# Two chained networks on one core: modulation weights taken in groups of four 2048-column units, and eight units of layer two moved behind the first expert stage

## The chip, the cores and the metric

One core of one Trainium2 chip runs the whole program in one launch. The metric is the device time of that launch in microseconds, the median of several runs. All arithmetic is in 32-bit floating point, apart from one clearing of accumulators in bf16.

## The reference, cut to what matters

256 tokens of width 1024 pass through a network of two layers and then through a second network. Each layer first makes a modulation vector from a condition vector `c`, and uses its six parts as shifts, scales and gates:

```python
for layer in range(2):
    mod = silu(c) @ w_ada[layer] + b_ada[layer]          # 1024 x 6144
    sh1, sc1, g1, sh2, sc2, g2 = split(mod, 6)
    h = rms_norm(x, norm1_g[layer]) * (1 + sc1) + sh1
    mix = (dilated attention | spatial gating)(h)        # layer 0, weights ev_*
          (causal convolution | stick-breaking attention)(h)  # layer 1, weights od_*
    x = x + g1 * mix
    h = rms_norm(x, norm2_g[layer]) * (1 + sc2) + sh2
    x = x + g2 * experts(h)        # 16 experts, top 2 of one group per token
x = rms_norm(x, final_norm_g)
```

The second network has a modulation of its own (`w_c`, 1024 x 3072), a 1024 x 8192 input projection `w_in`, a gated recurrence, a neighbourhood attention and three output projections.

## The kernel before, in words

**The ring.** All large weights pass through a ring of six SBUF slots (`RING`, L34), each holding one unit of 4096 floats per partition, 2 MB (2,097,152 bytes). `stream()` (L99) lists the units in order; SyncE fetches them in that order (L407 to L445). Unit n goes into slot n % 6 and its fetch waits until unit n - 6 has been read (`read_wait`, L278). A unit of `ada`, `ev`, `od` or `in` is 512 columns wide over all 1024 rows (`layout`, L419), so that each partition receives eight pieces of 2 KB. An expert unit gives each partition one piece of 16 KB.

**The modulation.** 30 `ada` units (24 of `w_ada`, 6 of `w_c`) are computed one by one. Most are done by TensorE: `ada_main` (L510) makes 8 products of 512 columns, four of them side by side on 32 columns of the array each (recorded as 16 matmuls, since an fp32 product is two), into one PSUM bank. This bank holds 4 partial sums, each repeated on 32 partitions. ScalarE copies the bank to SBUF (`ada_part_copy`, L1228); `ada_columns` (L534) adds over the partitions and turns row into column with four products with a column of ones (8 recorded matmuls), and VectorE scales by 1/32 and adds the bias (`ada_cols`, L1759). Ten units (4 to 11, 28, 29; `SUMMED`, L118) are instead summed by VectorE, `modulate` (L1767): eight multiply-adds of 512 columns per unit; `summed_columns` (L546) makes their columns.

**Stage one** is everything ahead of the first expert loop. It fetches 30 units in this order: ada 0 to 3; ev0; ada 4; ev1; ada 5, 6; ev2; ada 7; ev4; ada 8; ev3; ada 9 to 17; evo0, evo1; ada 18 to 22. TensorE's order is written out by hand: four `ada_main` with their columns (L613 to L632), the projections ev0, ev1, ev2 (L950 to L955), then eight attention heads (`heads`, L700): in each head the scores of the next head, the transposes of this head's probabilities (`turn`), and the value products (`values`). Head 0 holds ev4 ahead of its `turn`, head 1 holds ev3 and `summed_columns(8, 12)`. Heads 1 to 6 hold one `ada_main` between `turn` and `values` (`beside_turned`, L980) and one `ada_columns` behind `values` (`after_a`, L984): ada 12 to 17. Then follow evo0, evo1, two `ada_main`, and the routing of the experts.

**The routing** (`experts`, L714 to L763) is a chain between TensorE and VectorE (`route`, L1931). TensorE fills its waits: `units - 3` times `ada_main` and two `ada_columns` behind the logits, one `ada_main` and two (layer one) or one (layer two) `ada_columns` behind the rank products, and only then the product that counts tokens left over (L753) and the first `gather`.

**The expert loop** takes pairs of experts, six units per pair; the same in both layers.

**Stage two**, behind the first loop: od0, od1, od2, od3, od4, ada 23, odo0, odo1, ada 24 to 27. VectorE meanwhile runs the 31 taps of a causal convolution (`taps`, L2320) on od0 and od1. GpSimd sends the gate and two modulation rows through DRAM as 4-byte elements (`broadcast_gate`, L2584, `affine_by_row`, L2570): in layer one once 6 and 10 units are ready (L2643 to L2645), in layer two both right after unit 18 and the gain (L2661 to L2664).

## Time and profile before

| | us |
|---|---|
| median of 3 runs | 1254.09 |
| lowest and highest run | 1247.88, 1258.9 |
| span of the profiled execution | 1250.4 |
| TensorE busy in it | 1181.6 (94%) |
| VectorE, ScalarE, GpSimd busy | 417.0, 289.5, 83.6 |
| mean granted TensorE clock | 0.977 |
| DMA moved | 352.78 MB, mean 282 GB/s |

The span runs from the first to the last instruction of one execution taken by the profiler; no other time of that execution is given. PE is TensorE's matmul stream, PEld its weight loads, DVE VectorE, ACT ScalarE, POOL GpSimd, SP SyncE. L491 is a projection by channel, L504 one by token, L529 the products of `ada_main`, L542 those of `ada_columns`, L805 the experts' products, L777 the gather. A row names what ended the idle time before it behind `<-`.

### The profile page before, as it was taken

What the parts mean: (1) busy time and instruction counts of PE and PEld (TensorE: products, weight loads), DVE (VectorE), ACT (ScalarE), POOL (GpSimd) and SP (SyncE); (2) the same over time, 40 slices, a digit from 0 to 9 for tenths busy, and PEclk for the clock granted to TensorE, in tenths of its full rate; (3) what the DMA queues carried; (4) which work ended last, traced back from release to release, by engine and by line L of the source; (5) the groups of instructions that cost most, each with busy time, mean ns of one, the idle gap of its engine ahead of it and who ended that gap; (6) DMA issues with size and microseconds to landing.
All of it is one profiled execution on the core that took longest, in us unless ns stands there. A gap on an engine that the chain in (4) does not pass through costs nothing.

```text
span 1250.4 us, 17188 instructions
## 1 busy us (share of the span) xinstructions
PE 1181.6 (94%) x6994; PEld 696.9 (56%) x6995; DVE 417.0 (33%) x1096; ACT 289.5 (23%) x616; POOL 83.6 (7%) x141
## 2 busy tenths in 40 slices
PE   4979999999999989999989999998999999999997
PEld 1746644544444438764534443444877787767783
DVE  0456724322212123962521211114521243342222
ACT  2201433111000022063310001103002455452101
POOL 0200011000000001500000000000000223200000
PEclk8989889899999999999899999999999999999999
DMA  9999998899999999731769999999595334334000
GB/s 339 348 349 303 386 295 339 322 423 430 428 429 428 429 398 234 232 142 68 317 244 424 429 428 429 429 428 389 186 272 173 116 113 156 101 131 141 7 18 34
DMA packets 90372, 352.78 MB, mean 282 GB/s; under 512 B 5284, under 2 KB 7500, under 8 KB 78028
## 3 DMA queue, kind: packets, MB, share of 16 engines
q1 hardware_dynamic: 83160, 340.68, 72.2%
q0 software_dynamic: 5488, 8.12, 3.0%
q10 hardware_dynamic: 1668, 3.21, 0.7%
q8 instruction: 38, 0.62, 0.2%
q14 instruction: 18, 0.15, 0.0%
HBM read 350.84 MB, written 1.15 MB: 281 GB/s over the span
## 4 chain that ended last, share of the span: by engine, by line
PE 72%; DMA 20%; DVE 3%; ACT 2%; issue 1%; SPq 1%; DVEq 0%; ACTq 0%
PE bank L491 26%; PE bank L805 19%; DMA ring<-in_moe_w_up 12%; PE bank L504 10%; DMA ring<-in_w_ada 6%; PE bank L777 3%; DMA ring<-in_ev_w_out 2%; PE bank L826 2%; PE bank L529 2%; PE bank L1070 1%; DVE arena L1598 1%; SPq L401 1%; PE bank L542 1%; PE bank L655 1%; PE bank L692 1%
## 5 line engine op out<-in xcount | busy, mean ns | idle before, releaser
L491 PE MATMUL bank<-arena,ring 128*128 128x256 f32 x1600 | 353.6, 382 | 2.3 <-ACT arena L1163 1.7
L805 PE MATMUL bank<-ring,arena 128*32 128x512 f32 x3072 | 336.3, 595 | 10.3 <-issue 4.6
L491 PEld LDWEIGHTS bank<-arena,ring 128*128 128x128 f32 x1600 | 303.8, 191 | 49.3 <-issue 6.6
L805 PEld LDWEIGHTS bank<-ring,arena 128*32 128x32 f32 x3072 | 100.7, 110 | 233.4 <-issue 230.6
L504 PE MATMUL bank<-ring,arena 128*128 128x512 f32 x352 | 158.5, 608 | 11.3 <-DMA ring<-in_ev_w_in 8.1
L504 PEld LDWEIGHTS bank<-ring,arena 128*128 128x128 f32 x352 | 68.0, 195 | 93.7 <-issue 83.7
L2086 DVE TENSOR_TENSOR arena<-arena,bank 128x512 f32<-128x512 f32 x16 | 11.0, 688 | 200.1 <-PE bank L805 200.1
L777 PEld LDWEIGHTS bank<-arena 128*128 128x128 f32 x512 | 60.7, 198 | 11.7 <-issue 11.7
L777 PE MATMUL bank<-arena 128*128 128x128 f32 x512 | 63.6, 284 | 0.0
L1241 ACT ACTIVATE arena<-bank 128x512 f32<-128x512 f32 x41 | 23.5, 593 | 154.8 <-PE bank L491 111.4
L1345 ACT ACTIVATE arena<-bank 128x512 f32<-128x512 f32 x16 | 9.6, 597 | 211.3 <-PE bank L805 211.3
L1598 DVE SCALAR_TENSOR_TENSOR arena<-arena,cv 128x256 f32<-128x256 f32 x144 | 58.3, 480 | 0.3
L1601 DVE CUSTOM_DVE_ANT_1 arena<-bank,arena 128x256 f32<-128x256 f32 x32 | 12.3, 422 | 136.6 <-PE bank L656 136.6
L826 PE MATMUL bank<-arena 128*128 128x512 f32 x128 | 57.7, 594 | 0.0
L1337 ACT ACTIVATE arena<-bank,mod,gs 128x128 f32<-128x128 f32 x64 | 24.1, 456 | 128.0 <-PE bank L777 128.0
L529 PE MATMUL bank<-ring,c_rep 128*32 128x512 f32 x320 | 46.7, 716 | 7.1 <-DMA ring<-in_w_ada 5.2
L1598 DVE SCALAR_TENSOR_TENSOR arena<-ring,c_rep,arena 128x512 f32<-128x512 f32 x63 | 47.4, 752 | 2.2
L2072 DVE TENSOR_SCALAR arena<-bank,gs,mod 128x128 f32<-128x128 f32 x64 | 21.9, 405 | 51.4 <-PE bank L777 51.4
L1167 ACT ACTIVATE arena<-x 128x512 f32<-128x512 f32 x20 | 12.5, 626 | 111.9 <-DVE x L1811 95.4
L826 PEld LDWEIGHTS bank<-arena 128*128 128x128 f32 x128 | 23.2, 191 | 23.0 <-issue 23.0
L1264 ACT ACTIVATE arena<-arena,small 128x256 f32<-128x256 f32 (+1 forms) x48 | 22.4, 482 | 58.4 <-DVE small L1843 58.3
L1300 ACT COPY arena<-bank 64x256 f32<-64x256 f32 x32 | 11.7, 366 | 101.1 <-PE bank L693 92.2
(309 smaller groups left out, 922.6 us busy)
## 6 DMA issues: line engine op xcount, KB each, us to landing
ring<-in_moe_w_gate SPq DMA_DIRECT2D x32, 2048.0 KB, 14.8
ring<-in_moe_w_up SPq DMA_DIRECT2D x32, 2048.0 KB, 17.2
ring<-in_moe_w_down SPq DMA_DIRECT2D x32, 2048.0 KB, 13.2
ring<-in_w_ada SPq DMA_DIRECT2D x24, 2048.0 KB, 20.2
ring<-in_w_in SPq DMA_DIRECT2D x16, 2048.0 KB, 10.9
ring<-in_w_c SPq DMA_DIRECT2D x6, 2048.0 KB, 11.4
ring<-in_ev_w_in SPq DMA_DIRECT2D x5, 2048.0 KB, 21.8
ring<-in_od_w_in SPq DMA_DIRECT2D x5, 2048.0 KB, 19.8
```

The lines of the kernel that those rows point to most:

```text
L401: eng.dma_start(stage[r % P:r % P + n, r // P, :], src).then_inc(sem(f"{which}_loaded"), 16)
L491: mm = pe.matmul(ps[k0][:, t * S:(t + 1) * S], w[:, k, c:c + P], rhs[:, k, :], start=(k == 0), stop=(k == KT - 1))
L504: mm = pe.matmul(ps[k0][:, :], lhs[:, k, b * P:(b + 1) * P], w[:, k, :], start=(i == 0), stop=(i == KT - 1))
L529: mm = pe.matmul(bank[32 * g:32 * g + 32, :], c_rep[:, n // (2 * ADA_SEG), 4 * r + g, :], w[:, 4 * r + g, :], start=(r == 0), stop=(r == 1 ...
L777: mm = pe.matmul(ps[6 + b][:, (k % 4) * P:(k % 4 + 1) * P], xn[:, t, k * P:(k + 1) * P], pick[:, t, :], start=(t == 0), stop=(t == TT - 1))
L805: mm = pe.matmul(bank[col:col + CHUNK, :], lhs[:, k, col:col + CHUNK], ring[:, s0 + e, cut], start=start, stop=stop, tile_position=(0, col))
L826: mm = pe.matmul(ps[2 * t + half][:, :], g_cur[:, t * P:(t + 1) * P], y_pair[:, half * 512:(half + 1) * 512], start=False, stop=True, skip ...
L1241: act.activation(dst, v, func, scale=scale).then_inc(free, 1)
L1264: ins = act.activation(p[:, m * S:m * S + width[m]], p[:, m * S:m * S + width[m]], ACT.Exp, bias=small[:, c:c + 1], **kw)
L1337: ins = act.activation(x_cur[:, k, :], ps[6][:, k * P:(k + 1) * P], ACT.Identity, bias=mod[:, sh + k:sh + k + 1], scale=gs[:, 2 * layer + ...
L1598: return dve.scalar_tensor_tensor(out_, in0, scalar, in1, op0, op1)
L2072: ins = dve.tensor_scalar(x_cur[:, k, :], ps[7][:, (k - 4) * P:(k - 3) * P], gs[:, 2 * layer + 1, 0, k:k + 1], mod[:, sh + k:sh + k + 1], ...
```

## The change

Modulation units 0 to 27 are now cut the other way: four units make a group of 2048 columns, and each unit holds 256 of the 1024 rows, so that a partition receives two pieces of 8 KB. The four units of a group add into one bank (`group_main`, the same 8 products per unit), and a group has one copy, one set of four products that take 4 columns of the identity at once in place of one column of ones (8 recorded matmuls per group instead of per unit), and one addition on VectorE. Units 4 to 11 are still summed by VectorE, in two multiply-adds of 2048 columns per unit. The order of units, of TensorE's and ScalarE's steps and of GpSimd's sends changes with it. Units 12 to 15 are the only ones of TensorE's behind the first four in stage one; units 16 to 23 stand between the od projections.

```diff
     u = [("ada", n) for n in range(4)]
-    u += [("ev", 0), ("ada", 4), ("ev", 1), ("ada", 5), ("ada", 6), ("ev", 2), ("ada", 7)]
-    u += [("ev", 4), ("ada", 8), ("ev", 3), ("ada", 9)]
-    u += [("ada", n) for n in range(10, 18)]
+    u += [("ev", 0), ("ev", 1)]
+    u += [("ada", n) for n in range(4, 8)]
+    u += [("ev", 2), ("ada", 8), ("ada", 9), ("ev", 4), ("ada", 10), ("ada", 11), ("ev", 3)]
     u += [("evo", 0), ("evo", 1)]
-    u += [("ada", n) for n in range(18, 23)]
+    u += [("ada", n) for n in range(12, 16)]
     u += [("moe", 0)] * (6 * PAIRS)
-    u += [("od", i) for i in range(5)]
-    u += [("ada", 23), ("odo", 0), ("odo", 1)]
+    u += [("od", 0), ("od", 1)]
+    u += [("ada", n) for n in range(16, 20)]
+    u += [("od", 2), ("od", 3)]
+    u += [("ada", n) for n in range(20, 24)]
+    u += [("od", 4), ("odo", 0), ("odo", 1)]
     u += [("ada", n) for n in range(24, 28)]
...
+SUMMED_GROUPS, ROUTED_GROUPS = (1, 2), (3, 6)
...
+                        r, c0 = i % 4, 2048 * (i % ADA_SEG // 4)
+                        fetch(n, w[256 * r:256 * r + 256, c0:c0 + 2048].rearrange("(k p) c -> p k c", p=P))
...
+            def group_main(group, parts=range(4)):
+                bank, side = group_bank(group), group // 6
+                for r in parts:
+                    w = weights(2048)
+                    if r == 0 and group in (0, 6):
+                        pe.wait_ge(sem("setup_ready"), 4 if group else 1)
+                    elif r == 0:
+                        pe.wait_ge(sem("ada_ready"), 4 * group)
+                    for k in (2 * r, 2 * r + 1):
+                        for g in range(4):
+                            mm = pe.matmul(bank[32 * g:32 * g + 32, :], c_rep[:, side, k, :],
+                                           w[:, k % 2, 512 * g:512 * g + 512], start=(k == 0), stop=(k == KT - 1),
+                                           tile_position=(0, 32 * g))
+                    mm.then_inc(unit_done, 1)
+            one_of_32 = ident.rearrange("p (g r) -> p r g", r=32)[:, 0, :]
+            def group_columns(group):
+                part = group_part(group)
+                pe.wait_ge(sem("ada_part_taken"), copied_at(group))
                 for c in range(4):
+                    mm = pe.matmul(ps[4][:, 4 * c:4 * c + 4], part[:, c * P:(c + 1) * P], one_of_32,
                                    start=True, stop=True)
...
                 gate_row(gate, 1)
-                for n in range(units - 3):
-                    ada_main()
-                pe.wait_ge(sem("ada_part_taken"), copied_at(units_before + units - 2))
-                for n in range(2):
-                    ada_columns()
+                group_main(group, (2, 3))
...
-                ada_main()
-                for n in range(2, ROUTE_SOON[layer]):
-                    ada_columns()
+                pe.wait_ge(sem("ada_part_taken"), copied_at(group))
                 pe.wait_ge(sem("over_ready"), layer + 1)
...
-            by_token("ev2", hT, lambda: summed_columns(4, 6))
-            summed_columns(6, 8)
+            by_token("ev2", hT)
+            summed_group_columns(1)
...
-                    summed_columns(8, 12)
+                    summed_group_columns(2)
...
-            heads(0, 8, "dilated", between_a, after_a, beside_turned)
+            heads(0, 8, "dilated", between_a)
...
-            for name in ("od1", "od2", "od3"):
-                by_channel(name, hT)
+            by_channel("od1", hT)
+            group_main(4)
+            by_channel("od2", hT)
+            group_columns(4)
+            by_channel("od3", hT)
+            group_main(5)
...
             by_token("od4", hT, first_scores)
-            ada_main()
+            group_columns(5)
             taken(pe, "od4")
             scores(3, 0, "stick")
             turn(8, "stick")
-            ada_columns()
...
                 turned_probs(h, 384)
-                if 1 <= h < 7:
-                    ada_part_copy()
                 head_out(h, h, 0)
...
             take("ev0", 1, qT[:, 2:4, :], 0.125)
-            for n in (4, 5, 6):
+            for n in (5, 6, 7):
                 modulate(n)
             take("ev1", 1, kT[:, 2:4, :])
-            modulate(7)
-            summed_cols(4, 6)
-            modulate(8)
+            for n in (8, 9):
+                modulate(n)
             take("ev2", 1, v_tok[:, 1, :])
+            group_cols(1)
...
-            taps(2, 0, 20)
+            taps(2, 0, 10)
+            group_cols(4)
+            taps(2, 10, 20)
...
-            pool.wait_ge(sem("ada_ready"), 6)
+            pool.wait_ge(sem("ada_ready"), 8)
             broadcast_gate(0, mod[:, 16:24])
...
-            pool.wait_ge(sem("ada_ready"), 18)
-            pool.wait_ge(sem("gain_ready"), 4)
+            pool.wait_ge(sem("ada_ready"), 20)
             broadcast_gate(1, mod[:, 64:72])
-            affine_by_row(1)
             step(pool.memset(rg_w[:, :, :, :], 0.0))
             step.wait()
             for n in range(2):
                 load_bias(n)
                 load_gates(n)
+            affine_by_row(1)
```

`modulate(4)` now stands ahead of ev0's second half on VectorE. ScalarE's copies follow the groups: group 0 ahead of the first state, group 3 and 6 in the routing behind its second exponential, group 4 behind od1, group 5 behind od3. `group_cols` and the gain of the next norm stand inside `state_norm` behind each expert loop. Stage one now holds 23 units instead of 30, and the ring slot in `chunks` (L805) is taken modulo 6.

## Rows read from the trace of the kernel before

**Rows 1.** The page's part 4: the chain that ended last, by engine and line
```profile
PE bank L491 26%; PE bank L805 19%; DMA ring<-in_moe_w_up 12%; PE bank L504 10%; DMA ring<-in_w_ada 6%; PE bank L777 3%; DMA ring<-in_ev_w_out 2%; PE bank L826 2%; PE bank L529 2%; PE bank L1070 1%; DVE arena L1598 1%; SPq L401 1%; PE bank L542 1%; PE bank L655 1%; PE bank L692 1%
```

**Rows 2.** The chain that ended last, in order of time: start us, us, what
```profile
142.80 28.26 DMA ring<-in_ev_w_out
...
469.40 55.49 PE bank L491 x256
...
540.32 1.85 PE bank L529 x16
```

**Rows 3.** Timeline of VectorE, stage one: start us, us, operation, [idle before <-releaser]
```profile
71.84 0.49 DVE L1776 TENSOR_SCALAR arena<-ring,c_rep 128x512 f32<-128x512 f32 x1 [4.43 <-DMA ring<-in_w_ada]
...
93.53 0.49 DVE L1776 TENSOR_SCALAR arena<-ring,c_rep 128x512 f32<-128x512 f32 x1 [4.78 <-DMA ring<-in_w_ada]
...
113.44 0.49 DVE L1776 TENSOR_SCALAR arena<-ring,c_rep 128x512 f32<-128x512 f32 x1 [7.11 <-DMA ring<-in_w_ada]
...
113.96 5.48 DVE L1598 SCALAR_TENSOR_TENSOR arena<-ring,c_rep,arena 128x512 f32<-128x512 f32 x7
```

**Rows 4.** Busy time by window: after the busy times TensorE's granted clock, DMA share, GB/s
```profile
36.00:40.00 4.00, 1.92 (x12) 1.79 (x13) 2.36 (x7) 2.39 (x6) 0.00 (x0) 1.00 0.45 122
...
166.00:170.00 4.00, 2.37 (x17) 1.67 (x15) 0.78 (x5) 1.85 (x6) 0.00 (x0) 0.99 0.55 162
...
170.00:177.00 7.00, 5.69 (x7) 2.46 (x8) 0.00 (x0) 3.09 (x8) 2.52 (x4) 0.52 0.99 314
...
340.00:360.00 20.00, 20.00 (x187) 6.04 (x180) 2.98 (x6) 0.60 (x1) 0.00 (x0) 1.00 1.01 428
...
469.00:540.00 71.00, 70.60 (x300) 55.85 (x300) 48.90 (x126) 13.51 (x24) 18.93 (x31) 1.00 0.81 208
```

**Rows 5.** Timeline of TensorE: ev2, ev3, values of head 1, evo0
```profile
77.28 9.04 PE L504 MATMUL bank<-ring,arena 128*128 128x512 f32 x16 [8.12 <-DMA ring<-in_ev_w_in]
...
114.67 14.08 PE L491 MATMUL bank<-arena,ring 128*128 128x256 f32 x64
...
138.12 1.11 PE L695 MATMUL bank<-arena 128*64 128x256 f32 x2
...
171.31 27.82 PE L504 MATMUL bank<-ring,arena 128*128 128x512 f32 x58 [2.37 <-DMA ring<-in_ev_w_out]
```

**Rows 6.** Timeline of TensorE, then of ScalarE: one head of the first attention
```profile
140.94 0.38 PE L649 MATMUL bank<-arena 64*128 64x128 f32 x2
...
141.72 1.92 PE L529 MATMUL bank<-ring,c_rep 128*32 128x512 f32 x16
...
143.59 0.65 PE L695 MATMUL bank<-arena 128*64 128x256 f32 x2
...
144.39 1.05 PE L542 MATMUL bank<-kc,ada_part 128*128 128x1 f32 x8
...
142.24 0.80 ACT L1264 ACTIVATE arena<-arena,small 128x256 f32<-128x256 f32 x2 [1.04 <-DVE small L1843]
...
143.06 0.48 ACT L1293 COPY arena<-bank 128x384 f32<-128x384 f32 x1
...
144.49 0.37 ACT L1300 COPY arena<-bank 64x256 f32<-64x256 f32 x1 [0.20 <-PE bank L696]
```

**Rows 7.** Timeline of the routing: TensorE, ScalarE, VectorE, and TensorE in layer two
```profile
220.10 2.71 PE L529 MATMUL bank<-ring,c_rep 128*32 128x512 f32 x16
...
222.74 3.58 PE L542 MATMUL bank<-kc,arena 128*128 128x1 f32 x16
...
226.60 6.07 PE L777 MATMUL bank<-arena 128*128 128x128 f32 x32
...
216.54 0.21 ACT L1329 ACTIVATE arena<-arena 128x2 f32<-128x2 f32 x1
...
223.29 0.42 DVE L2054 TENSOR_TENSOR arena<-arena 128x256 f32<-128x256 f32 x1
...
621.78 3.82 PE L777 MATMUL bank<-arena 128*128 128x128 f32 x32
```

More of the change, by code:

```diff
@@ L272, in summed_at, with last_of, copied_at @@
             return sum(summed_unit(u) for u in units[:n + 1])
-        def copied_at(n):
-            return sum(m not in SUMMED for m in range(n + 1))
+        def last_of(group):
+            return unit_of[f"ada{4 * group + 3}"]
+        def copied_at(group):
+            return sum(g not in SUMMED_GROUPS for g in range(group + 1))
         def read_wait(eng, n):
@@ L629, in _ @@
             turn_x()
-            ada_columns()
-            ada_main()
-            ada_columns()
+            group_main(0, (3,))
+            group_columns(0)
             head = [0]
@@ L698, in values, with heads @@
                 mm.then_inc(sem("o_full"), 1)
-            def heads(lo, hi, kind, between, after=lambda h: None, mid=lambda h: None):
+            def heads(lo, hi, kind, between):
                 base = head[0]
@@ L891, in experts @@
                     by_split(pe.snap(split_reg), pair)
-                ada_columns()
+                group_columns(group)
                 to_next = pe.mark_branch_hint_location()
@@ L999, in _ @@
             by_token("evo1", oT, arrived=first_tile(1))
-            for n in range(2):
-                ada_main()
+            group_main(3, (0, 1))
             turn_tile(1, 1)
@@ L1046, in _ @@
             by_token("odo1", oT, arrived=first_tile(3))
-            for n in range(2):
-                ada_main()
+            group_main(6, (0, 1))
             turn_tile(3, 1)
@@ L1712, in state_norm @@
                     pre_root(1, no, 4 * no + 3)
+                group_cols(ROUTED_GROUPS[r // 2 - 1])
+                gain(r)
                 inverse(1, no)
@@ L2341, in _ @@
             softplus()
-            ada_cols()
+            group_cols(5)
+            gain(3)
             for h in range(8):
```

223 lines of the change are left out of this document (84 added, 139 removed).

## The prediction

> **What bounds the kernel now.** I read the page's chain first, then the chain in order of time, then timelines and windows of the stages that the diff touches. The chain by line [rows 1] is TensorE's products, with loads between them: the experts' loads 12%, `w_ada` 6%, `ev_w_out` 2%. In order of time [rows 2] the last of these waits in stage one is for evo0's weights; stage two is an unbroken run of projections (469.4, 55.49 us) with one modulation unit on the chain at 540.32. So the change takes loads out of a stage that waits for loads, and puts TensorE work into one that waits for TensorE. The question is how much of stage one's wait it gets back.
>
> Stage one is less bound by loads than [rows 2] make it look. TensorE waits for a unit in two places only: 8.12 us ahead of ev2 [rows 5] and 2.37 us ahead of evo0 (168.94 to 171.31) [rows 5]. Between them lie eight heads, a chain through TensorE, VectorE and ScalarE.
>
> **What a unit costs to load.** VectorE starts on ada 6 and ada 8 as each lands, at 71.84 and 93.53; the stream has four units from the one to the other: 21.69 us, 5.42 for a unit of 2 KB pieces [rows 3]. Ada 8 to ada 9, two units, takes 19.91 instead of 10.84, so 9.07 us are lost there; the 4-byte sends of `broadcast_gate(0)` lie in that stretch. Expert units (16 KB pieces) go at 428 GB/s [rows 4], 2.097 MB / 428 = 4.90 us. A unit of 8 KB pieces isn't in the trace: between 4.90 and 5.42. The 0.52 us between the two forms is 56 fewer pieces on each of 16 DMA engines (64 against 8), 9.3 ns each; 16 pieces give 4.97, my value, 0.45 below today. The Trainium skill ("DMA: Bandwidth & Descriptors", Bandwidth) puts about 10.5 ns on a packet; by it the unit would take 4.92, an estimate. Its rule in the section on rules for kernel authors, 128 partitions and at least 1 MiB for full bandwidth, would give no gain at all from 8 KB pieces, since all these units are 2 MB; the step from 5.42 to 4.90 speaks against that.
>
> **Stage one, step by step.** *ev2* was unit 10 and becomes unit 11: + 4.97, - 7 units x 0.45 = 3.15, - 2.2 for the hole in the stream at 36 to 40 us (4 us at a share of 0.45 [rows 4], while small rows are issued; fewer pieces should close it). Sum -0.4, with ends -1.6 (4.90) and +3.2 (5.42). The wait ahead of ev2 stays as it is: ev0 and ev1 fill TensorE up to then in both.
> *ev3* wasn't waited for. It becomes unit 17, where ada 9, the 15th, landed at 113.44: + 9.94, - 10 x 0.45, - 2.2, at about 116.7. TensorE today starts it at 114.67 [rows 5], so it now waits 2 us, and on top loses some 1.7 to the low clock, as ev2 did after its wait (9.04 for its first half, against 7.04 for half of ev3 at full clock). VectorE's sums, about 6.0 us a unit today (0.49 + 5.48 [rows 3]), take 4.8 to 6.0 in two wide steps and end before ev3; today the three from 113.44 on end at 131.3. Behind ev3 come 16 column products as before, the layer norm and its root, and `values` of head 1 at 138.7, where it is today at 138.12 [rows 5], behind an `ada_main` at low clock. Up to head 2: +0.5, ends -3 and +5.
> *Heads 2 to 7* lose `ada_main` (1.92) and `ada_columns` (1.05). One head in [rows 6]: scores end at 141.32, the exponential of the next head runs 142.24 to 143.04, the copy of the transposed probabilities 143.06 to 143.54, and `values` starts at 143.59. `ada_main` at 141.72 to 143.64 lies beside that and hides nothing else: without it `values` starts at the same time. The columns (144.39 to 145.4) hide ScalarE's copy at 144.49 to 144.86, so only 0.45 of them comes out. Four such heads 1.8, the head with the mixing products 1.2 more, the tail 0.6: -3.6. But TensorE then works 2.1 us in 4.5. The window 170 to 177 shows 0.52 of full clock after a stretch with 2.37 us busy in 4 at full clock [rows 4]. At 1.2 GHz scores and `values` take 1.8 us longer per head, 9 over five; I take a third, +3, ends 0 and 9.
> The Trainium skill ("TensorE: Matmul & The Clock Gate", HAM oscillation) warns of just this, short bursts of products between waits that throw the clock down again and again; by it the whole 9 us are paid. Rows 4 show one such fall, not a repetition.
> *evo0* then starts at 169.3 instead of 171.3 (the load lands long before): -2.0. Up to 1.2 of the low clock behind the old wait (0.52 in 170 to 177) may go: I count 0.6.
> *Routing of layer one*: TensorE's `ada_main` (220.10) and columns (222.74, 3.58 us at low clock) go; `gather` started at 226.60, while VectorE's pick was ready at 223.71. ScalarE's copies ahead of the second exponential (216.54) go too, 0.8. So gather starts 3.7 earlier [rows 7]: -3.7, ends -4.5 and -2.
>
> Stage one: 0.5 - 3.6 + 3.0 = -0.1, less 1.9 of the wait ahead of evo0 (the head's last copy still takes 0.4), -0.6, -3.7: **-6.3**, ends -13 and +6.
>
> The expert loop has a full ring at its entry, and from its first released slot on it runs at the rate of its loads, DMA share 1.00 [rows 4]; its length doesn't change.
>
> **Stage two.** Eight units enter and one leaves, each 1.85 on the chain [rows 2]: 7 x 1.85 = +12.95. Columns: two sets enter, one leaves, 1.05 at most each [rows 6]: +1.0. TensorE is busy 70.6 of 71 us here at full clock [rows 4], so nothing hides them: **+13.9**, ends 12.5 and 15. Their loads have room (208 GB/s in that window): +0, at worst one loss of 9.1 as with the gate's sends above, since layer two's gate and rows are now sent later, beside od2 to od4. `group_cols(4)` waits on VectorE for columns that are there some 5 us before it comes to them; the taps behind it have slack against od4. GpSimd's row sends start after od4 and are needed only behind odo1.
> **Norms and routing of layer two**: VectorE's late columns move off, -0.3. The last `ada_main` and its columns go, gather could start 1 to 2 us earlier, but at low clock it takes 6.07 where it now takes 3.82 [rows 7]: 0, ends -1.5 and +1.5.
>
> **Sum.** -6.3 + 13.9 - 0.3 = +7.3. The profiled span is 1250.4 and lies 3.7 under the median of the runs, 1254.09; 1250.4 + 7.3 = 1257.7, plus 3.7: 1261. I round down to **1260**, since the low-clock term is the softest and only added. A difference under 1% (12.5 us) is about what a measurement of this kernel can't tell from none.
>
> **Rivals.**
> 1. *The heads' work comes out in full.* If each head shortens by `ada_main` and its columns, 2.9 x 6 = 17.2 instead of 3.6, with the clock held, evo0 starts 18.7 earlier (its load has landed by about 125). Sum -18.7 - 1.2 - 3.7 + 13.9 - 0.3 = -10.0: 1244. For it: [rows 1] have L529 on the chain with 2%. Against it: [rows 6], where `values` starts within 0.05 of the ScalarE copy. Chance 0.12.
> 2. *Low clock in the heads, ev3 late* (slower): all 9 us instead of 3, and ev3 at the 5.42 price, 5 later. It decides once heads and ev3 together lose 6 us more than I charge them. 1260 + 6 + 5 = 1271. For it: the fall at 170. Against it: at 1.2 GHz the share rises by itself. Chance 0.18.
> 3. *The moved loads aren't hidden*: od4 or a group in stage two waits behind the small sends, +9: 1269. Against it: 81% share and a ring six units deep there [rows 4]. Chance 0.08.
> 4. *Even*: stage one gives back all it is charged (clock holds, ev3 on time, the first routing in full): +13.9 - 0.3 - 13 = about nothing, 1254. Chance 0.10.
>
> **How the numbers follow.** The forecast has 0.52, with a range of its own of 1253 to 1266. The range 1247 to 1271 leaves out the lower half of rival 1 and the top of rival 2. Faster by over 1% (under 1241.5): half of rival 1, 0.06. Slower by over 1% (over 1266.6): most of rival 2, half of 3, a tail of the forecast, 0.23. Within 1%: 0.71.
>
> **What would show it.** Right: in the profile after, `values` of the heads still released by ScalarE's copy of the transposed probabilities, a head period near 4.5 to 5.4; no wait for evo0; gather of layer one ahead of the first expert product by the same 7 us but starting right behind VectorE's pick; the expert loop as long as before; 128 recorded L529-like matmuls in stage two at full clock and od0 to odo0 some 13.9 longer. Wrong: heads of 2 to 3 us; a wait for a load in stage two; first expert product of layer one earlier than 222 or later than 235 (before: 233.5).

## The result, and the profile after

The changed kernel takes 1272.28 us (median of 4 runs, 1271.37 to 1273.94) against 1253.58 us of the kernel before (4 runs, 1247.88 to 1258.9): ratio 1.0153, 95% interval 1.0116 to 1.0191. It is 1.5% slower; the forecast was 1260, with a range up to 1271. The profiled run (1271.37 us) has a span of 1269.7 us, 19.3 more than the 1250.4 of before.

First the page's parts 4 and 5 of the kernel after, which answer to [rows 1]: the chain by line, then the two costliest groups (busy, mean ns | idle time before them, what ended most of it).

```profile
PE bank L493 27%; PE bank L791 20%; PE bank L506 12%; DMA ring<-in_moe_w_up 10%; PE bank L763 3%; PE bank L812 2%; DMA ring<-in_ev_w_in 2%; DMA arena<-in_ev_w_s 2%; PE bank L1048 1%; PE bank L521 1%; PE bank L690 1%; PE bank L650 1%; PE bank L687 1%; PE bank L543 1%; PE bank L643 1%
...
L493 PE MATMUL bank<-arena,ring 128*128 128x256 f32 x1600 | 356.2, 384 | 7.1 <-issue 4.7
L791 PE MATMUL bank<-ring,arena 128*32 128x512 f32 x3072 | 338.0, 597 | 12.3 <-issue 7.2
```

`w_ada` has left the chain (6% before), and so has `ev_w_out` (2%). The wait ahead of ev2 is still there, now put down to ev2's own load. What came instead is more of TensorE's own work (the projections by token, L506, have 12% for 10%, those by channel, L493, 27% for 26%) and something that none of [rows 1] to [rows 7] warned of: "issue", time in which TensorE stands with nothing to wait for, 4.7 us ahead of the projections and 7.2 us ahead of the experts' products.

The chain in order of time (start us, us, what) says where:

```profile
78.94 16.55 PE bank L506 x32
95.49 4.44 PE bank L543 x32
...
101.51 15.49 PE bank L506 x32
...
120.28 14.01 PE bank L493 x64
...
230.52 13.87 PE bank L791 x128
...
257.03 2.39 issue
...
497.04 7.00 PE bank L521 x64
...
532.76 7.00 PE bank L521 x64
...
886.30 3.95 issue
```

Set against the same points of before, the 19.3 us come stage by stage as follows (in us, from the timelines of TensorE; evo0 of before is in [rows 5]).

| stretch | before | after | difference |
|---|---|---|---|
| start to evo0 | 171.3 | 174.6 | +3.2 |
| evo0 to first expert product, layer one | 62.2 | 56.0 | -6.2 |
| expert loop, layer one | 226.5 | 229.3 | +2.8 |
| end of the loop to od0 | 9.4 | 9.4 | 0 |
| od0 to odo0 (stage two) | 101.3 | 114.6 | +13.3 |
| odo0 to first expert product, layer two | 60.4 | 59.5 | -0.9 |
| expert loop, layer two | 228.7 | 230.3 | +1.7 |
| end of the loop to in0 | 12.0 | 16.7 | +4.7 |
| in0 to the end | 378.7 | 379.4 | +0.7 |

Three things stand out. Stage two pays 13.3, near the forecast 13.9. Stage one gives back 3.0 where 6.3 were forecast. And 7.1 us are stalls of TensorE in places where before has none: 2.39 us in the loop of layer one, which is nearly all of its +2.8, and 4.71 us ahead of in0. A stall at the entry of the loop of layer two is in both profiles: 4.58 us before, 3.74 and then 1.06 after. Because the later part falls behind the first product, the row from odo0 on looks 0.8 better and the loop of layer two 1.1 worse than they are. The +0.7 behind in0 is low clock: the 192 products there take 43.06 us where they took 42.34.

In the heads of before `values` came every 4.95 us (155.35, 160.30, 165.27; one head stands in [rows 6]). Here is the timeline of TensorE after, `values` of heads 1 and 3 to 7 and evo0, with what each waited for in brackets:

```profile
140.43 1.11 PE L690 MATMUL bank<-arena 128*64 128x256 f32 x2 [2.28 <-ACT arena L1264]
...
154.02 0.65 PE L690 MATMUL bank<-arena 128*64 128x256 f32 x2 [0.57 <-ACT arena L1264]
...
158.53 0.65 PE L690 MATMUL bank<-arena 128*64 128x256 f32 x2 [1.80 <-ACT arena L1264]
...
163.69 1.11 PE L690 MATMUL bank<-arena 128*64 128x256 f32 x2 [1.31 <-ACT arena L1264]
...
169.61 1.11 PE L690 MATMUL bank<-arena 128*64 128x256 f32 x2 [1.45 <-ACT arena L1264]
...
172.55 1.11 PE L690 MATMUL bank<-arena 128*64 128x256 f32 x2 [0.57 <-ACT arena L1264]
...
174.55 3.68 PE L506 MATMUL bank<-ring,arena 128*128 128x512 f32 x6 [0.46 <-ACT arena L1271]
```

The releaser is ScalarE's copy each time, as forecast, and evo0 waits for no load. Where `values` takes 0.65 us the head lasts 4.5 (154.02 to 158.53); where it takes 1.11, on the low clock, 5.9 (163.69 to 169.61).

The same stretch by windows (after the busy times: TensorE's granted clock, DMA share, GB/s), with the first loads and the stretch behind ev2 ahead of it:

```profile
32.00:36.00 4.00, 2.66 (x24) 1.23 (x16) 0.42 (x3) 0.67 (x2) 0.00 (x0) 1.00 0.70 255
36.00:40.00 4.00, 2.92 (x7) 2.42 (x8) 2.84 (x7) 3.45 (x7) 0.00 (x0) 0.54 0.71 233
...
84.00:98.00 14.00, 14.00 (x51) 7.61 (x49) 8.93 (x5) 1.88 (x2) 0.00 (x0) 0.99 1.03 407
98.00:104.00 6.00, 6.00 (x21) 4.22 (x21) 1.61 (x10) 0.80 (x2) 0.91 (x1) 0.50 1.01 407
139.00:152.00 13.00, 9.22 (x29) 6.40 (x30) 7.58 (x27) 4.67 (x10) 0.00 (x0) 0.50 0.62 259
153.00:159.00 6.00, 3.18 (x18) 1.98 (x16) 4.62 (x18) 2.12 (x5) 0.00 (x0) 1.00 0.00 0
160.00:174.00 14.00, 10.22 (x29) 5.97 (x29) 4.79 (x27) 3.65 (x9) 4.32 (x6) 0.50 0.11 2
```

TensorE's clock is at its lower level (0.50, 1.2 GHz) in both long parts of the heads and at the upper one (2.4 GHz) for a short time between. It is also low at 98 to 104, where before it was not; that is taken up below. From 32 to 40 the DMA engines are at 0.70 and 0.71, so the hole in the stream that before has from 36 to 40 (0.45, [rows 4]) didn't close. And the DMA engines do nothing from 153 to 159: there the loads are no longer what stage one waits for, and the time went to the chain through the heads.

### The profile page after: what moved, and what is told of

The parts are those of the page before. It is cut to its first block, busy times and chain, and to the rows that moved or that the text cites. A ratio compares the mean times of both kernels' runs of the same rounds, so it can differ in the third digit from the quotient of the medians.

```text
span 1269.7 us, 16862 instructions
## 1 busy us (share of the span) xinstructions
PE 1175.6 (93%) x6874; PEld 690.2 (54%) x6875; DVE 406.7 (32%) x1037; ACT 281.8 (22%) x601; POOL 84.7 (7%) x141
## 4 chain that ended last, share of the span: by engine, by line
PE 77%; DMA 14%; DVE 3%; ACT 3%; issue 2%; ACTq 0%; SPq 0%; DVEq 0%
PE bank L493 27%; PE bank L791 20%; PE bank L506 12%; DMA ring<-in_moe_w_up 10%; PE bank L763 3%; PE bank L812 2%; DMA ring<-in_ev_w_in 2%; DMA arena<-in_ev_w_s 2%; PE bank L1048 1%; PE bank L521 1%; PE bank L690 1%; PE bank L650 1%; PE bank L687 1%; PE bank L543 1%; PE bank L643 1%
## 5 line engine op out<-in xcount | busy, mean ns | idle before, releaser
L493 PE MATMUL bank<-arena,ring 128*128 128x256 f32 x1600 | 356.2, 384 | 7.1 <-issue 4.7
L493 PEld LDWEIGHTS bank<-arena,ring 128*128 128x128 f32 x1600 | 305.1, 192 | 55.4 <-issue 12.2
L506 PE MATMUL bank<-ring,arena 128*128 128x512 f32 x352 | 158.7, 609 | 11.8 <-DMA ring<-in_ev_w_in 10.5
L506 PEld LDWEIGHTS bank<-ring,arena 128*128 128x128 f32 x352 | 68.1, 196 | 95.9 <-issue 82.8
L1561 DVE SCALAR_TENSOR_TENSOR arena<-ring,c_rep,arena 128x2048 f32<-128x2048 f32 (+1 forms) x21 | 38.2, 1818 | 11.1 <-DMA ring<-in_w_ada 10.5
L521 PE MATMUL bank<-ring,c_rep 128*32 128x512 f32 x320 | 39.8, 641 | 0.9 <-ACT c_rep L1108 0.9
```

Source lines behind the costliest of these rows:

```text
L493: mm = pe.matmul(ps[k0][:, t * S:(t + 1) * S], w[:, k, c:c + P], rhs[:, k, :], start=(k == 0), stop=(k == KT - 1))
L506: mm = pe.matmul(ps[k0][:, :], lhs[:, k, b * P:(b + 1) * P], w[:, k, :], start=(i == 0), stop=(i == KT - 1))
L521: mm = pe.matmul(bank[32 * g:32 * g + 32, :], c_rep[:, side, k, :], w[:, k % 2, 512 * g:512 * g + 512], start=(k == 0), stop=(k == KT - 1) ...
L1561: return dve.scalar_tensor_tensor(out_, in0, scalar, in1, op0, op1)
```

## The experiments

**Is it the clock in the heads, and does the expert loop swallow what stage one gains?** The heads get products without use where the modulation stood before. (The edits are shown in short here and below; waits for a free bank and arguments are left out.)

```diff
+            def fill(count):
+                for g in range(count):
+                    pe.matmul(ps[4][32 * (g % 4):32 * (g % 4) + 32, :], c_rep[:, 0, g % KT, :],
+                              hT[:, 0:2, :].rearrange("p a b -> p (a b)"), ...)
...
                     turn(base + h - lo, kind)
+                    if 2 <= h < 8: fill(8)
```

> The kernel after, with eight extra products (32x512 each, into a bank nobody reads then) behind the transposes of heads 2 to 7, where the modulation products stood before. Theory A (the eight heads lost time to the low clock alone): the clock stays up in the heads, the period of a head falls from 5.9 us to 4.5 to 5.0, evo0 starts at 169 to 171 instead of 174.55. Theory B (the expert loop of layer one ends when its loads end, whatever its entry): the loop still ends at 459 to 460.5 and the whole takes 1272 +- 2. Rival of B: the earlier entry comes out in full, the loop ends 3.5 to 5 us earlier and the whole takes about 1268. Rival of A: the heads wait on something else; period and evo0 stay, or evo0 comes 5 us or more later by the extra 11 us of products.

Measured: 1261.52 us (5 runs, 1258.71 to 1268.04), ratio to before 1.0103 (1.0057 to 1.0149). Windows of this kernel:

```profile
153.00:159.00 6.00, 5.54 (x45) 2.28 (x43) 4.56 (x19) 1.75 (x5) 0.00 (x0) 1.00 0.00 0
160.00:174.00 14.00, 12.52 (x82) 5.46 (x81) 5.42 (x30) 5.27 (x14) 4.32 (x6) 1.00 0.09 3
```

Its timeline of TensorE:

```profile
154.92 0.65 PE L690 MATMUL bank<-arena 128*64 128x256 f32 x2
...
159.44 0.65 PE L690 MATMUL bank<-arena 128*64 128x256 f32 x2
...
168.53 0.65 PE L690 MATMUL bank<-arena 128*64 128x256 f32 x2
...
173.15 1.12 PE L506 MATMUL bank<-ring,arena 128*128 128x512 f32 x2 [0.46 <-ACT arena L1284]
```

Theory A holds for the heads: with work between them the clock stays up from 149 on, and a head lasts 4.5 us (154.92 to 159.44) although it holds 1.9 us more of products. The kernel after has the same 4.5 where its clock is up. The eight products of a unit are thus free in a head at the upper clock; what is left of the 4.95 of a head of before is, by difference, the columns. But evo0 comes only 1.4 us earlier (173.15), since head 2 runs its filler at the low clock and head 7 now has one too. Theory B falls: the loop of layer one lasts 226.5 us and ends at 456.4, 3.4 earlier. It is its length that stays, not its end. Most of what else the two profiles differ by isn't from the heads at all: this run has no stall in the loop of layer one (2.4 us) and none ahead of in0 (4.7).

**Taking the move back, half and whole.** half_back puts group 3 into heads 2 to 5 and group 4 beside the routing of layer one; all_back puts groups 3 and 4 into the heads, two units in a head, and group 5 beside that routing. The order of loads and the copies follow.

```diff
-SUMMED_GROUPS, ROUTED_GROUPS = (1, 2), (3, 6)
+SUMMED_GROUPS, ROUTED_GROUPS = (1, 2), (4, 6)        # half_back; (5, 6) in all_back
...
+                if 2 <= h < 6: group_main(3, (h - 2,))          # half_back
...
+                if h in (2, 3): group_main(3, (2 * h - 4, 2 * h - 3))     # all_back
+                elif h == 4: group_columns(3)
+                elif h in (5, 6): group_main(4, (2 * h - 10, 2 * h - 9))
+                elif h == 7: group_columns(4)
```

> Group 3 (four units) goes back into heads 2 to 5 of stage one, group 4 becomes the one beside the routing of layer one, so stage two keeps one group of the two. Theory A (stage two pays 1.85 us a unit on its chain, the heads hide a unit and its products keep the clock up): od0 to odo0 falls from 114.6 to about 108, evo0 comes 0 to 4 us earlier, the loop's end doesn't move; 1272 - 6.7 = 1265.6, 1262 to 1268. Rival 1 (a unit in the heads costs as much as in stage two): 1270 to 1275. Rival 2 (the stalls of TensorE that no wait explains, 2.4 us at 257 and 4.7 us ahead of in0, sit where they do by the layout of the program): they move or vanish here although nothing near them is changed, 1258 to 1263.

> Groups 3 and 4 (eight units) go back into the heads of stage one, two units in each of heads 2, 3, 5 and 6; group 5 stands beside the routing of layer one and stage two has none. The new grouping and its columns stay. Theory A (what the change lost is the move, 13.3 us in stage two): od0 to odo0 back to 100 to 101.5, evo0 at 172 to 177 (two units in a head are 3.8 us, more than one head hides), loop ends at 460; 1272 - 13.5 = 1258.5, 1254 to 1263. Rival 1 (the wide grouping itself costs what the early part of stage one lost and more): 1264 to 1272. Rival 2 (grouping is worth its saved columns and copies): under 1252. If the unexplained stalls vanish too, 4 to 7 us less than each of these.

Measured: half_back 1266.96 us (ratio 1.0128, 1.01 to 1.0157), all_back 1257.6 us (10 runs, 1253.23 to 1260.91; ratio 1.0026, 0.9994 to 1.0057). All_back can't be told from before. In it od0 to odo0 is 99.3 us: 15.3 less than after, and 2 less than before, as it has one unit less there. The heads pay for two units at a time: evo0 starts at 181.50, 7 us later than after. The stall ahead of in0 is there with 4.73, and one of 1.13 in the loop of layer one. Half_back, with one unit in each of four heads, needs 32.8 us from `values` of head 1 to evo0 (137.45 to 170.21) against 34.1 in the kernel after (140.43 to 174.55): rival 1 of half_back falls. At the upper clock a head with a unit lasts 4.51 us (152.21 to 156.72), so a single unit costs a head nothing. Its stage two reads

```profile
468.28 58.34 PE L492 MATMUL bank<-arena,ring 128*128 128x256 f32 x256 [5.57 <-issue]
```

in the timeline of TensorE: the four projections take 58.34 us where they took 55.49 [rows 2], because they start behind a stall of 5.57 us and on the low clock. So here a stall came ahead of od0, where neither before nor after had one, and the one ahead of in0 (4.62) is there as well. The stall ahead of od0 and the slower projections behind it cost half_back 8.4 us in this profile, and all_back has neither; how long half_back takes without them was not tried.

**What is late ahead of evo0?** Two kernels look at ev2 and what follows. ev2_warm puts 28 products without use ahead of TensorE's wait for ev2; group1_pe gives group 1 to TensorE in that wait, with a copy by ScalarE and four column products, instead of VectorE's sums and 16 products of one column in one run.

```diff
             by_channel("ev1", hT)
+            fill(28)                          # ev2_warm
             by_token("ev2", hT)
...
             by_channel("ev1", hT)
+            group_main(1)                     # group1_pe
             by_token("ev2", hT)
-            summed_group_columns(1)
+            group_columns(1)
```

> The kernel after, with 28 extra products (32x512, into a free bank) ahead of TensorE's wait for ev2, to keep its clock up through that wait. Theory A (evo0 comes late since ev2 and what follows start on the low clock): ev2 takes 14.1 us instead of 16.55, the columns behind it 3.4 or less instead of 4.44, ev3 starts at 116.5 to 117.5 (its load lands at 116.4) instead of 120.28, evo0 at 170 to 172. Whole: 1272 +- 2 if the expert loop's end is set by its loads, 1269 if not. Rival (the clock falls anyway, or the order of loads sets ev4 and ev3): evo0 at 174 to 175.5.

> The kernel after, with group 1 taken from VectorE (sums, 16 column products of one column) and given to TensorE (32 products in its 10.5 us of waiting ahead of ev2, then four column products). Theory A (the 16 column products behind ev2, 3.6 us in which TensorE does little, throw the clock down for ev4): columns 0.8 to 1.6 us instead of 4.6, no fall of the clock at 97.8, ev4 14.0 to 14.5 us instead of 15.54 and from 96.5 to 97.5 on, ev3 bound by its load (116.4) instead of 120.21, evo0 at 170 to 171.5: whole 1272 - 4 = 1268. Rival: group 1's last unit lands with ev2, so that TensorE has its products (1.9 us) between ev2's landing and ev2: evo0 at 173 to 175, whole 1271 to 1273.

Measured: ev2_warm 1269.56 us (1.0151, 1.0122 to 1.0181), group1_pe 1272.22 us (1.0162, 1.0111 to 1.0212). The timeline of TensorE in ev2_warm:

```profile
78.87 15.44 PE L506 MATMUL bank<-ring,arena 128*128 128x512 f32 x32 [3.02 <-DMA ring<-in_ev_w_in]
94.15 3.63 PE L543 MATMUL bank<-kc,arena 128*128 128x1 f32 x32
...
98.56 15.70 PE L506 MATMUL bank<-ring,arena 128*128 128x512 f32 x32
...
117.48 14.08 PE L493 MATMUL bank<-arena,ring 128*128 128x256 f32 x64
```

and in group1_pe:

```profile
93.53 0.95 PE L533 MATMUL bank<-kc,ada_part 128*128 128x4 f32 x8
...
95.27 14.00 PE L506 MATMUL bank<-ring,arena 128*128 128x512 f32 x32
...
116.46 16.87 PE L493 MATMUL bank<-arena,ring 128*128 128x256 f32 x64 [3.90 <-DMA ring<-in_ev_w_in]
```

with these windows:

```profile
98.00:104.00 6.00, 6.00 (x16) 2.65 (x15) 4.96 (x17) 2.68 (x4) 0.00 (x0) 1.00 1.19 197
```

In ev2_warm ev2 takes 15.44 us, not the 14.1 expected: the 28 products end 3.02 us ahead of it. ev4 still takes 15.70. In group1_pe ev2 takes 15.44 as well, but the one-column products are gone, the clock stays at 1.00 from 98 to 104 and ev4 takes 14.00. The two differ in what stands between ev2 and ev4, so the run of 3.6 us of one-column products (in the kernel before, two halves of 1.84 with half of ev2 between them) is what costs ev4 1.5 us or more. The gain is not kept: ev3's load lands only at 116.46, where the prediction had it (116.7), ev3 then waits 3.90 us and starts cold. evo0 starts at 171.96 and 174.65 in them, and both stall ahead of od0, by 5.23 and 5.29 us, and not ahead of in0. ev2_warm's 2.6 us are no proof of its edit: the unedited kernel, profiled again below, had evo0 at 172.88.

**Where do the stalls come from?** So far five kernels had different sets of them. The unedited kernel was profiled again (after_again), and with 24 products of one column in the wait ahead of ev2, meant only to move the later instructions 96 places on.

```diff
             by_channel("ev1", hT)
+            for n in range(24):               # pad; 48 in pad48
+                pe.matmul(ps[4][:, 0:1], hT[:, 0, 0:P], ones[:, 0:1], start=True, stop=True)
             by_token("ev2", hT)
```

> The changed kernel itself, unedited, profiled once more. So far TensorE stood without a wait that the profile shows for 2.39 us in the loop of layer one, 3.74 us at the entry of the loop of layer two and 4.71 us ahead of in0; the four edited kernels showed 5.57 or 5.23 us ahead of od0 in two cases, none ahead of in0 in two, none in the loop of layer one in all four. Theory L (the place of each stall is a property of the program): the same three stalls at the same places, within 0.5 us. Theory R (each execution draws them anew): at least one of the three is missing, or one appears ahead of od0. The rest of the milestones (evo0 174.5, first expert products 230.5 and 643.2) within 1 us but for such stalls.

> The kernel after, with 24 products of one column (96 more TensorE instructions, some 3 us) in TensorE's 10.5 us of waiting ahead of ev2. They take no time from anything, but every later instruction of TensorE stands 96 places further. Theory L (place in the program decides): the stalls without a wait change their set, as they did in the edited kernels: at least one of the three goes or one appears ahead of od0, evo0 as before to within 0.5 us. Theory R (drawn anew): any set, as after_again shows for the unedited one. If after_again and this one both have exactly the three stalls of the kernel after, neither holds, and what the edits changed near the branches is the cause.

Measured: after_again 1272.01 us with 2.31 us in the loop of layer one, 3.49 at the entry of the loop of layer two and 4.83 ahead of in0: the same three. (all_back, told above, had 1.13 in the loop of layer one, so "none in all four" isn't right.) pad 1269.71 us with 5.42 us ahead of od0, 3.93 at that entry, 1.17 further on in the loop of layer two, none ahead of in0 and none in the loop of layer one. The first is as theory L has it; the second fits it, but doesn't exclude theory R. evo0 was 172.88 and 172.12 against 174.55, further off than either expectation allowed (1 and 0.5 us).

The two edits that looked good were then put together, and 48 products were tried, which theory L says must give the set of heads_filled.

> The two edits together: groups 3 and 4 in the heads, group 5 beside the routing of layer one, and group 1 on TensorE ahead of ev2. If the edits add: 1257.6 - 4 = 1253.6, 1251 to 1256, evo0 at 177 to 178 (181.5 in the one alone). Rival (the heads are filled by ten more us of products and their start is set by ev3's load anyway): 1256 to 1258.

> The kernel after, with 48 products of one column in TensorE's wait ahead of ev2: 192 more TensorE instructions, as many as heads_filled has ahead of the loops. Theory L (the place in the program decides where TensorE stands without a wait): the set of heads_filled, that is 3.8 us at the entry of the loop of layer two and none in the loop of layer one, ahead of od0 or ahead of in0, although neither the kernel after (two runs) nor the one with 24 such products shows that set. Then the whole takes 1272 - 2.4 - 4.8 = 1264.8, 1262 to 1266, and that part of the 18.7 us that the change costs is chance of layout. Theory R, or a cause in the code near the branches: the stalls of the kernel after or of pad, 1269 to 1273.

> all_back_group1 with 28 products of one column in TensorE's 5.4 us of waiting ahead of ev3: 112 more instructions, which puts the loop of layer two where heads_filled has it and the end of the loop of layer one between places that showed no stall. Theory L: the 5.37 us ahead of od0 (and the low clock behind it, 2.5 us) go and nothing appears ahead of in0: 1260.6 - 7.5 = 1253, 1251 to 1255, no different from the kernel before. Rival: the stalls stay, 1259 to 1262; or they move to in0, 1256 to 1258.

Measured: all_back_group1 1260.63 us (1.0081, 1.0055 to 1.0106): evo0 came at 178.6 instead of 181.5, near the 177 to 178 expected, but a stall of 5.37 us stood ahead of od0, which ate it. all_back_group1_placed 1265.0 us (6 runs, 1261.32 to 1275.28; 1.0114, 1.0063 to 1.0164): the stall ahead of od0 stayed, 5.57, so that placing failed, and the 28 products took 9.1 us where TensorE had 5.4 to spare, so that ev3 came at 120.97 instead of 117.56. pad48 1270.52 us (9 runs, 1263.22 to 1277.56; 1.0138, 1.0099 to 1.0177): 4.68 us ahead of in0, not the set of heads_filled; its 48 products took 15.5 us and made ev2 4.4 us late. Theory L in its strict form falls. So one last pair:

```diff
-                to_next = pe.mark_branch_hint_location()
                 results(PAIRS - 1)
                 scatter(PAIRS - 1)
+                to_next = pe.mark_branch_hint_location()      # hint_late
```

> The kernel with 48 one-column products once more, unedited. Its nine times fall into 1263.2 to 1266.2 (four) and 1270.5 to 1277.6 (five), and its profile, of a run of 1270.5, shows 4.68 us ahead of in0 in which TensorE's page of instructions is fetched only inside the gap. Theory M (place and chance: whether a page comes in time differs between executions of one program): a time near 1264 comes with no stall ahead of in0, a time near 1271 with one. Theory L in its strict form (place alone): the same 4.7 us, at either time.

> The kernel after with TensorE's branch hint for the jump past the leftover code given 17 instructions later, behind the last scatter of the expert loop. Theory F (the stall ahead of in0 is the fetch of the page jumped to, and the hint decides when it starts): the 4.7 us ahead of in0 change, to 0 if the hint came too early to be kept (1272 - 4.7 = 1267), to about the same or 1 us more if it came too late, and the fetch is seen in the wait before the transposes' product instead of inside the gap. Rival (the hint has nothing to do with it): 4.7 us at the same place, 1272.

pad48_again took 1270.33 us, and the same program now stalls elsewhere, which neither theory as put there had: not ahead of in0, but ahead of od0. Timelines of TensorE, first pad48, at od0 and in0:

```profile
469.44 1.75 PE L493 MATMUL bank<-arena,ring 128*128 128x256 f32 x7 [0.67 <-ACT arena L1166]
...
889.07 1.19 PE L493 MATMUL bank<-arena,ring 128*128 128x256 f32 x2 [4.68 <-issue]
```

and pad48_again:

```profile
472.67 1.62 PE L493 MATMUL bank<-arena,ring 128*128 128x256 f32 x3 [5.33 <-issue]
...
890.00 1.52 PE L493 MATMUL bank<-arena,ring 128*128 128x256 f32 x3
```

What differs is when instructions come. They have DMA queues of their own. The one that goes with TensorE's stalls is q8, whose part in the page after is 36 packets and 0.59 MB, 16.4 KB each. Packets by queue in windows of pad48, first 872 to 884 (the last scatter and the transposes ahead of in0), then 884 to 889 (the gap):

```profile
q1 hardware_dynamic: 2302, 4.64, 105.2%
...
q1 hardware_dynamic: 943, 1.90, 103.2%
q8 instruction: 1, 0.02, 1.3%
```

and of heads_filled, 869 to 880, all of it ahead of in0 (880.72), which didn't stall:

```profile
q1 hardware_dynamic: 2103, 4.24, 104.6%
q8 instruction: 1, 0.02, 0.6%
```

With the stall, no packet of q8 comes until TensorE stands. Without it, one came at 873.33, at the end of the last scatter and ahead of the transposes (877.19). The traces of all 16 profiles say the same. They hold 32 starts of od0 or in0, 13 of them behind a stall of 4.62 to 5.57 us. In all 13 a packet of q8 starts 1.9 to 2.9 us after TensorE has stopped, and the first product follows 2.7 or 2.8 us behind the packet's start. In the 19 others it either starts 4.8 to 7.7 us ahead of the first product (11), or there is none until about 2 us behind that product (8). That makes these 13 stalls waits for a page of instructions behind a jump (od0 and in0 both stand behind the jump over the code for left-over tokens), and pad48 twice shows that place and chance both have a part. For the stall in the loop of layer one it isn't shown: there the packet ends 0.1 to 0.4 us before the gap begins. The Trainium skill ("Runtime: NRT & Kernel Launch", Instruction fetch mechanics) says that instructions are refilled in blocks of 16 KiB and that a taken branch whose target isn't in the window held forces a fetch before execution can go on; the trace agrees in the size of the packets and in the place of the fetch.

hint_late (1272.65 us; 1.0172, 1.0129 to 1.0215) has 4.94 ahead of in0: moving the hint by 17 instructions changed nothing, and what decides whether the page comes in time stays open.

**Does the kernel before have them too?** It was profiled twice more.

> The kernel before, unedited, profiled once more. Its one profile has a single stall of TensorE without a wait, 4.58 us at the entry of the loop of layer two, which all kernels have; its times spread over 1242 to 1268. Theory M (pages of instructions come late by place and by chance, and the changed kernel's place ahead of in0 is a bad one): no stall ahead of in0 or in the loop of layer one here either, though one ahead of od0 may come, with a time 5 to 7 us higher. Rival (chance alone): the stalls of 4.7 us ahead of in0 or 2.4 us in the loop show up here as well, and then they are no part of what the change costs.

> The same once more, for the same question: with three profiles of each kernel the stalls ahead of in0 stand 3 of 3 (the changed kernel, counting the one with the later hint) against 0 of 3 by theory M, and against 1 or 2 of 3 by chance alone.

Measured: 1242.52 and 1243.53 us. No stall ahead of od0 or in0, none in the loop; 4.79 and 4.20 at the entry of the loop of layer two. But the surprise is elsewhere: timelines of TensorE in before_again, evo0, the second transposes' columns and the gather of layer one, to be held against [rows 5] and [rows 7]:

```profile
167.40 25.16 PE L504 MATMUL bank<-ring,arena 128*128 128x512 f32 x58 [0.46 <-ACT arena L1300]
...
213.52 1.92 PE L529 MATMUL bank<-ring,c_rep 128*32 128x512 f32 x16
215.37 1.95 PE L542 MATMUL bank<-kc,arena 128*128 128x1 f32 x16
...
217.41 5.45 PE L777 MATMUL bank<-arena 128*128 128x128 f32 x32
```

In the profile that I predicted from, evo0 waited 2.37 us for its load, ran partly on the low clock (27.82 us) and the routing's late products did too (2.71 and 3.58 instead of 1.92 and 1.95). In before_again evo0 doesn't wait for its load; in before_third it does for 0.88 us, takes 26.83 and is followed by 3.54 and 1.99 in the routing, so a part of the low clock is there as well. evo0 starts at 167.4 and 168.3 in the two; evo0 to the first expert product takes 56.2 and 57.9 us, not 62.2. Three profiles of each kernel, in us (the third of after is hint_late, whose code differs by the place of that hint alone):

| stretch | before | after |
|---|---|---|
| start to evo0 | 171.3, 167.4, 168.3 | 174.6, 172.9, 174.7 |
| evo0 to first expert product | 62.2, 56.2, 57.9 | 56.0, 56.3, 56.1 |
| loop, layer one | 226.5, 226.3, 226.2 | 229.3, 227.5, 228.1 |
| od0 to odo0 | 101.3, 101.3, 101.3 | 114.6, 114.6, 115.6 |
| end of loop two to in0 | 12.0, 12.0, 12.0 | 16.7, 16.8, 16.9 |

So the stall ahead of in0 is there in 3 of 3 profiles of the one and in 0 of 3 of the other, that in the loop of layer one likewise (2.39, 2.31, 2.04). The ten profiles of the edited kernels other than hint_late stall ahead of od0 or in0 in nine cases, heads_filled alone in neither. That is theory M, and a part of what this change costs, though nothing in its purpose; three profiles of before are few to say that it never stalls there.

The table also says that the 3.0 us that stage one gave back depend on the profile of before. First expert product: 233.5, 223.6 and 226.3 before, 230.5, 229.2 and 230.8 after. Against the two later profiles stage one got slower. These two were short executions (1242.5 and 1243.5 us, with a median of 1253.58 for the kernel), so the first one is the more typical, but which of its waits are the kernel's stays open.

## Why the prediction was wrong

- **Stage two, +13.9: right.** 13.3 measured; L521 stands on the chain twice for 7.00 us (1.75 a unit, not 1.85), the columns for 0.79. No load was late there, so rival 3 didn't come; all_back takes it back.
- **evo0 -2.0 (with the low clock behind it -2.6): wrong, +3.2.** Three terms failed.
  - *ev2 -0.4* was +1.7 (78.94 against 77.28). The price of a unit held (4.96 to 4.98 us against 4.97), but the hole in the stream, charged with -2.2, didn't close: the DMA share is 0.70 and 0.71 from 32 to 40, 2.4 us lost where before lost 2.2. (The term's own lower end was worked out wrongly too: with 4.90 us a unit it gives -0.9, not -1.6.)
  - *Up to head 2 +0.5* was +2.3 (140.43 against 138.12, [rows 5]). I had ev3 held up by its load alone, at 116.7. The load did land at 116.4, but TensorE came later, at 120.2: ev2 started late, and from there to ev3 it took 41.3 us where it took 37.4 before. "Behind ev3 come 16 column products as before" was said of group 2; that the same 16 products in one run stand behind ev2, without half of ev2 between them, wasn't priced, and they put ev4 on the low clock (15.49 us against 14.00).
  - *The low clock in the heads, +3 of 9*, was mis-sized. From `values` of head 1 to `values` of head 7 the heads took 32.1 us (140.43 to 172.55) against 29.95 before (138.12 to 168.07). If the work that comes out saved the 3.6 forecast, the low clock gave back that and 2.2 more: 5.8 of the 9. Head by head, against the heads of heads_filled and half_back at the upper clock, it comes to about 5, an estimate.
  - Rival 2 had asked for all 9 and a late ev3; of its 11 us 2.8 and 1.8 came true. The Trainium skill's rule on the oscillation of the clock ("TensorE: Matmul & The Clock Gate", HAM oscillation), which I had weighed down to a third, was right in that the fall comes back (in its case TensorE waits for loads, in these heads for ScalarE): low from 139 to 152 and again from 160 to 174, up between. The price taken from it, all 9, was about as far off as mine.
- **The wait ahead of evo0 goes: right**, and so was the head's releaser. But in the two later profiles of before there was little or no wait to lose (0.88 us and none).
- **Routing of layer one, -3.7: right for the profile it was made from**, 6.2 with evo0's clock against 4.3 forecast. Against the two later profiles of before it is about 0 to -1.9: what left was mainly low clock of that one execution. Of the work taken out, ScalarE's copies count 0.8 (TensorE waits 2.06 us for VectorE where before_again spent 2.9 on its columns and waits); the rest lay beside VectorE's pick.
- **"Its length doesn't change", of the expert loop: right but for a stall**: 226.2 to 227.3 us in layer one in all other profiles, 229.3, 227.5 and 228.1 in the three with the stall of 2.0 to 2.4 us. I had no term for TensorE standing without a wait, though the page of before has 4.6 us of issue ahead of the experts' products, which I did not take up.
- **Norms and routing of layer two**: -0.9 against -0.3; within its ends, and 0.8 of it is the stall at the loop's entry, which moved partly into the loop. The gather starts 2.3 us earlier behind odo0 and takes 2.2 longer on the low clock, much as forecast.
- **The end: +4.7 ahead of in0, +1.7 in loop two, +0.7 after; forecast 0.** The prediction has no term for this part and gives no reason for that. What the runs showed in their place: TensorE stands 4.71 us ahead of in0 until a page of instructions has come. This is what carried the time over the range. In sum: forecast +7.3; stage one 3.3 worse, stalls 7.1, the rest 1.6 worse, total 19.3.

The forecast's sign and its main term held. It missed by a term that wasn't in it (the stalls), by one that was weighed too lightly (the clock in the heads), and by two on the way to ev3 (the hole in the stream, the one-column products behind ev2).

No kernel tried beats the one before: all_back is even with it, at 1257.6.

## What to carry to other kernels

Work taken out of a chain that runs between engines isn't only hidden work: it keeps TensorE's clock up, and here its products cost a head nothing, while the same products in a stretch that TensorE fills cost their full 1.75 us a unit. Before pricing a term from one profile, ask which of its waits and low-clock stretches are the execution's and not the kernel's; a term made of these alone can be nothing. Give a change that moves instructions around loops and jumps a margin of some 5 to 7 us on kernels of this size for instruction pages that come late, and look for "issue" in the chain before looking for any other cause.

## What the runs showed of the hardware that I had not expected

- A jump over code can cost 4.6 to 5.6 us if its page of instructions is fetched only when TensorE stands, in one place in one execution and in another in the next of the same program, and the low clock behind it costs 2.5 to 2.9 more at od0 (od0 to odo0 117.1 in pad against 114.6; the four projections of half_back 58.34 against 55.49) and 0.7 to 2.4 at in0 (192 products in 43.06 us in after and 44.70 in hint_late against 42.34).
- 16 products of one column (3.6 us in one run) let TensorE's clock fall behind them, and in the kernel before it falls too where they stand in one run, behind ev3: the eight products of 512 columns that follow without a wait take 3.40 us in before_again and 2.99 in before_third, not 1.92. Four products of four columns (0.95 us) didn't, and neither did two runs of 1.84 us with half of ev2 between them.
- Products of one column aren't free, and TensorE that is busy with them alone isn't kept warm. 24 in a row took 5.63 us in pad, 0.23 each, as long as one of 512 columns (1.92 for eight). In pad48 the granted clock fell to a mean of 0.68 under 48 of them, although matrix and weight loads were busy throughout (its windows; busy times, then clock, DMA share, GB/s):

```profile
68.00:83.00 15.00, 15.00 (x96) 15.00 (x94) 8.00 (x5) 0.00 (x0) 0.00 (x0) 0.68 1.02 382
```

- Units of 8 KB pieces came 4.96 and 4.98 us apart where nothing else was sent, against 5.42 for units of 2 KB pieces [rows 3] and the forecast 4.97. In VectorE's timeline after, ada 8 is taken at 83.90 and ada 9 at 88.88 (ev2 at 78.94 ahead of both):

```profile
83.90 1.29 DVE L1731 TENSOR_SCALAR arena<-ring,c_rep 128x2048 f32<-128x2048 f32 x1 [5.04 <-DMA ring<-in_w_ada]
...
88.88 4.74 DVE L1561 SCALAR_TENSOR_TENSOR arena<-ring,c_rep,arena 128x2048 f32<-128x2048 f32 x2 [1.31 <-DMA ring<-in_w_ada]
```
